# Expert stage: second layer two pairs behind the first, its result transposes beside the gather's

## The reference

```python
h = _layernorm(x) * (1.0 + sc2) + sh2
f = _moe_ffn(h, router_w, router_b, exp_w1, exp_w3, exp_w2, sh_w1, sh_w3, sh_w2)
x = _layernorm(DN_ALPHA * x + g2 * f, ln2_w, ln2_b)
```

## Time and profile before

| | |
|---|---|
| median of 3 runs | 2037.02 us (2030.13 to 2043.91) |
| profiled execution, first to last instruction | 2023.2 us |
| mean granted TensorE clock | 0.955 of full speed |
| TensorE busy | 1867.4 us, 92% of the span |
| VectorE, ScalarE, POOL busy | 980.9, 647.1, 331.0 us |
| first-layer matmuls (L3467), 1536 of them | 343.6 us |
| second-layer matmuls (L3451), 768 of them | 176.8 us |
| first matmul of the first pair, end of the last pair | 1381.4 us, 1980.6 us |

### The profile page before, as it was taken

The page is one execution under the profiler, slowest core; times in us unless marked ns, Lnnn a source line. Parts: engine busy times, 40 slices in busy tenths (PEclk is TensorE's granted clock), DMA queues, the critical chain, the costliest instruction groups (busy, mean ns, idle before and its releaser), DMA issues.

```text
span 2023.2 us, 33529 instructions
## 1 busy us (share of the span) xinstructions
PE 1867.4 (92%) x14234; PEld 1338.9 (66%) x14234; DVE 980.9 (48%) x1446; ACT 647.1 (32%) x1012; POOL 331.0 (16%) x316
## 2 busy tenths in 40 slices
PE   7989998999997999899999789979899999999991
PEld 6878998999997999765755679874333333333330
DVE  5745555465664677746545754663232222222116
ACT  5544334444454433420033532422111112111110
POOL 2100000000000100012200025402133233233323
PEclk9989999999998999999899789979999999999996
DMA  8534555544443877446497000076999999999885
GB/s 278 189 105 157 186 187 187 164 147 147 151 141 121 296 249 249 148 149 185 148 343 250 1 14 4 4 298 264 420 391 366 373 370 367 377 371 374 328 328 200
DMA packets 199700, 456.49 MB, mean 226 GB/s; under 512 B 33048, under 2 KB 154392, under 8 KB 170000
## 3 DMA queue, kind: packets, MB, share of 16 engines
q1 hardware_dynamic: 157104, 377.18, 51.8%
q0 software_dynamic: 35712, 57.73, 8.4%
q10 hardware_dynamic: 6752, 19.67, 2.7%
HBM read 549.91 MB, written 52.43 MB: 298 GB/s over the span
## 4 chain that ended last, share of the span: by engine, by line
PE 81%; DVE 8%; DMA 4%; issue 3%; ACT 3%; POOL 1%; SPq 0%; ACTq 0%; POOLq 0%; DVEq 0%
PE psum L349 32%; PE psum L3467 15%; PE psum L3451 7%; PE psum L1570 7%; PE psum L1577 2%; PE psum L3393 2%; DMA mem<-in_exp_w_dram 2%; PE psum L2607 2%; ACT w_hi L405 1%; PE psum L2591 1%; DVE w_lo L410 1%; DMA mem<-in_exp_w_dram,mem 1%; PE psum L3480 1%; PE psum L569 1%; PE psum L3150 1%
## 5 line engine op out<-in xcount | busy, mean ns | idle before, releaser
L410 DVE TENSOR_TENSOR w_lo<-mem,w_hi 128x2048 fp32r<-128x2048 f32 x122 | 280.2, 2299 | 228.0 <-ACT w_hi L405 225.4
L349 PE MATMUL psum<-x_hi,w_hi 128*128 128x256 f32 x1216 | 349.0, 287 | 4.3 <-DVE x_lo L556 4.3
L3467 PE MATMUL psum<-mem 128*64 128x512 f32 x1536 | 343.6, 600 | 6.1 <-DMA mem<-in_exp_w_dram 3.6
L349 PE MATMUL psum<-x_hi,w_lo 128*128 128x256 f32 x1216 | 343.9, 283 | 0.0
L349 PE MATMUL psum<-x_lo,w_hi 128*128 128x256 f32 x1216 | 342.9, 282 | 0.0
L405 ACT ACTIVATE w_hi<-mem 128x2048 fp32r<-128x2048 f32 x122 | 233.9, 1918 | 192.9 <-PE psum L349 189.8
L3467 PEld LDWEIGHTS psum<-mem 128*64 128x64 f32 x1536 | 106.8, 138 | 204.4 <-issue 195.0
L349 PEld LDWEIGHTS psum<-x_hi,w_hi 128*128 128x128 f32 x1216 | 233.2, 192 | 10.1 <-DVE w_lo L410 4.7
L349 PEld LDWEIGHTS psum<-x_lo,w_hi 128*128 128x128 f32 x1216 | 236.7, 195 | 0.6
L349 PEld LDWEIGHTS psum<-x_hi,w_lo 128*128 128x128 f32 x1216 | 235.7, 194 | 0.0
L3451 PE MATMUL psum<-mem 128*64 128x512 f32 x768 | 176.8, 602 | 4.2 <-issue 3.0
(11 more groups left out here) (512 smaller groups left out, 2848.9 us busy)
## 6 DMA issues: line engine op xcount, KB each, us to landing
mem<-in_exp_w_dram SPq DMA_DIRECT2D x192, 1024.0 KB
mem<-in_dil_w_qkv_dram SPq DMA_DIRECT2D x36, 1024.0 KB, 5.3
mem<-in_ada_w_dram POOLq DMA_DIRECT2D x48, 512.0 KB, 4.2
mem<-in_ffn_w_gate_dram SPq DMA_DIRECT2D x22, 1024.0 KB, 5.6
mem<-in_ffn_w_up_dram SPq DMA_DIRECT2D x22, 1024.0 KB, 5.6
mem<-in_ffn_w_down_dram SPq DMA_DIRECT2D x22, 1024.0 KB, 4.7
mem<-in_w_in_dram SPq DMA_DIRECT2D x13, 1024.0 KB, 5.5
mem<-in_na_w_qkv_dram SPq DMA_DIRECT2D x12, 1024.0 KB, 8.4
```

Source lines behind the costliest of these rows:

```text
L349: ins = pe.matmul(out, lhs[a], rhs[b], start=start and k == 0, stop=stop and k == 2, **kw)
L410: dve.tensor_tensor(w_lo[n % SLOTS][:, 0, :], ring[:, n % SLOTS, :], w_hi_f[n % HI][:, 0, :], ALU.subtract).then_inc(S("w_split"), 1)
L3467: ins = pe.matmul(psum[r, up, :].rearrange("p (a n) -> p a n", a=2), xg[:, b % 2, c, x * P + 64 * e:x * P + 64 * e + 64], w_up[s][e][:, :, ...
```

## The change

The second layer runs two pairs behind the first. In iteration k TensorE now runs the first layer of pair k, then at once the two result transposes of pair k-1 (`turned(k - 1)`), then the 8 gather transposes, then the second layer of pair k-2. `hid_T` gets a second buffer. VectorE copies the turned result of pair k-1 ahead of the product of pair k. All that belongs to the second layer moves along: SP issues, behind the first-layer loads of pair k, the second-layer loads of pair k-2 (it was k-1), POOL likewise for spare pairs, and `y_put` and `y_out` come an iteration or two later. The last two pairs are written out by hand.

```diff
-    hid_T = gain_b[:, 512:768].rearrange("p (c j) -> p c j", c=2)
+    hid_T = [gain_b[:, 512 + 256 * q:768 + 256 * q].rearrange("p (c j) -> p c j", c=2) for q in range(2)]
...
-        for k, (kind, n) in enumerate(PAIRS + [("end", 0)]):
+        for k, (kind, n) in enumerate(PAIRS + 2 * [("end", 0)]):
...
-            elif k >= 3 and PAIRS[k - 1][0] == "own":
-                sp.wait_ge(*at("mx_y", k - 2))
-                down_rows(k - 1, PAIRS[k - 1][1], range(2))
+            elif k >= 4 and PAIRS[k - 2][0] == "own":
+                sp.wait_ge(*at("mx_y", k - 3))
+                down_rows(k - 2, PAIRS[k - 2][1], range(2))
...
-            if k > 2 and PAIRS[k - 1][0] == "spare":
-                fetch_down(k - 1, PAIRS[k - 1][1])
+            if k > 3 and PAIRS[k - 2][0] == "spare":
+                fetch_down(k - 2, PAIRS[k - 2][1])
...
-            if k - 3 >= PLAIN:
-                y_put(pool, k - 3)
-        y_put(pool, len(PAIRS) - 3)
+            if k - 4 >= PLAIN:
+                y_put(pool, k - 4)
+        for k in range(len(PAIRS) - 4, len(PAIRS) - 2):
+            y_put(pool, k)
...
+        def turned(k):
+            pe.wait_ge(*at("mx_hid", k + 1))
+            after(pe, "hid_T", k)
+            if k == 0:
+                pe.wait_ge(*at("spare_rows", 3))
+            for f in range(2):
+                ins = pe.transpose(bank(1, P, f * P), hid_tok[:, f::2], ident)
+            ins.then_inc(S("hid_turned"), 1)
...
             ins.then_inc(S("mx_up"), 1)
+            if 0 < k < last:
+                turned(k - 1)
             if b + 1 < BATCHES:
                 for u in range(2):
                     gather_pe(pe, b + 1, 2 * x + u)
-            if k:
-                down(k - 1)
-            pe.wait_ge(*at("mx_hid", k + 1))
...
-            for f in range(2):
-                ins = pe.transpose(bank(1, P, f * P), hid_tok[:, f::2], ident)
-            ins.then_inc(S("hid_turned"), 1)
             if k == 0:
                 slot_toks_pe(pe, 2)
-        down(len(PAIRS) - 1)
+            if 2 <= k < last:
+                down(k - 2)
+            if k == last - 1:
+                turned(k)
+                down(k - 1)
+        down(last - 1)
+        turned(last)
+        down(last)
...
-            if k == 1:
+            if k == 3:
                 act.wait_ge(*at("y_filled", 16 * FILLS))
-            if 0 < k <= PLAIN:
-                y_out(act, k - 1)
+            if 3 <= k < 3 + PLAIN:
+                y_out(act, k - 3)
...
+        def hid_turned(k):
+            dve.wait_ge(*at("hid_turned", k + 1))
+            after(dve, "mx_y", k - 1)
+            dve.tensor_copy(hid_T[k % 2], bank(1, 256).rearrange("p (c j) -> p c j", c=2)).then_inc(S("hid_T"), 1)
+
         for k in range(len(PAIRS)):
             b, x = divmod(k, 2)
+            if 0 < k < last:
+                hid_turned(k - 1)
             dve.wait_ge(*at("mx_silu", k + 1))
             after(dve, "hid_turned", k)
             dve.tensor_tensor(hid_tok, sil, bank((0, 6)[k % 2], 256, 256), ALU.mult).then_inc(S("mx_hid"), 1)
-            if k:
+            if 2 <= k < last:
+                y_dve(dve, k - 2)
+            if k == last - 1:
+                hid_turned(k)
                 y_dve(dve, k - 1)
```

More of the change, by code:

```diff
@@ L3450, in down @@
                         r = slice(64 * e, 64 * e + 64)
-                        ins = pe.matmul(psum[r, 4 + h, :], hid_T[:, f, r], w_down[s][e][:, f, 512 * h:512 * h + 512],
+                        ins = pe.matmul(psum[r, 4 + h, :], hid_T[s][:, f, r], w_down[s][e][:, f, 512 * h:512 * h + 512],
                                         start=f == 0, stop=f == 1)
             ins.then_inc(S("mx_y"), 1)
+        def turned(k):
[6 more added lines that the diff above has]
+            ins.then_inc(S("hid_turned"), 1)
+        last = len(PAIRS) - 1
         for k in range(len(PAIRS)):
@@ L3473, in moe_pe @@
                     gather_pe(pe, b + 1, 2 * x + u)
-            if k:
-                down(k - 1)
-            pe.wait_ge(*at("mx_hid", k + 1))
-            if k == 0:
-                pe.wait_ge(*at("spare_rows", 3))
-            for f in range(2):
-                ins = pe.transpose(bank(1, P, f * P), hid_tok[:, f::2], ident)
-            ins.then_inc(S("hid_turned"), 1)
             if k == 0:
                 slot_toks_pe(pe, 2)
-        down(len(PAIRS) - 1)
+            if 2 <= k < last:
[6 more added lines that the diff above has]
+        down(last)
     def xg_act(act, b, u):
@@ L3548, in moe_dve @@
             dve.tensor_tensor(hid_tok, sil, bank((0, 6)[k % 2], 256, 256), ALU.mult).then_inc(S("mx_hid"), 1)
-            if k:
+            if 2 <= k < last:
+                y_dve(dve, k - 2)
+            if k == last - 1:
+                hid_turned(k)
                 y_dve(dve, k - 1)
-            dve.wait_ge(*at("hid_turned", k + 1))
-            after(dve, "mx_y", k)
-            dve.tensor_copy(hid_T, bank(1, 256).rearrange("p (c j) -> p c j", c=2)).then_inc(S("hid_T"), 1)
             if k == 0:
@@ L3564, in moe_dve @@
                 gate_dve(dve, k - 2)
-        y_dve(dve, len(PAIRS) - 1)
+        y_dve(dve, last - 1)
+        hid_turned(last)
+        y_dve(dve, last)
         for r in range(3):
```

## The result

The changed kernel takes 2040.7 us, the median of 20 runs, against 2030.8 us for the kernel before, also of 20. The ratio is 1.0054, with a 95% interval of 1.0036 to 1.0072: half a per cent slower, 11 us. (Three of the forty, at 2196 us and more, ran in a slow state and are left out of the ratio.) The forecast had the direction and the place, and three times the size: +34 us. (The three runs shown before the change had a median of 2037.0; with twenty it is 2030.8. A profiled execution of the changed kernel took 2040.27 us with a span of 2038.1, so what lies around the span is 2.2 us, not the 13.8 that I took over; the execution profiled before was a quick one: 2.2 us on its span of 2023.2 give 2025.4.)

The account below looks back on a forecast made before the run. TensorE's instructions were taken to bound the kernel, loads close behind. Load-loop and end terms of +25.0 us plus +9.4 for the clock gave +34 on the 2023.2 us span; with a 13.8 us offset, 2071 us, range 2038 to 2092.

Parts of the forecast that it names:

- The drains saved on TensorE: On TensorE between second and next first layer: 0.36 us saved on about 26 of 48 pairs, 9.4 us if TensorE stays the bound.
- The first rival: Turns of three pairs: ten loads land within 27.5 us, no wait appears, 9.4 us gained, 2028 us; chance 0.12.
- the second, the loop without the clock: Every third first layer: waits of 1.7 to 3.0 us, full clock, turns of 37.7 to 39.0 us, 2045 to 2062 us; chance 0.28.
- the signs that I named: Middle stretch: waits about 3 us every third pair, turns 38 to 41 us, TensorE share about 0.92, clock below 1.00.
- 30.4 + 1.4 us: Load loop of each turn: ten loads, 10.49 MB at 0.345 MB a us, 30.4 us, plus 1.4 for start and landing.
- My lower bound: Load loop of each turn: ten loads packed without a gap, with q0's small packets, take 29.2 us, a turn of 37.7.
- The upper bound of 41.5: Load loop of each turn: a 3.9 us tail at the end of the loads makes a turn 41.5 us.
- a small gain behind up(40): After pair 40's first layer, with fewer loads: TensorE saves 4 x 0.36 = 1.4 us.
- the clock at the 11 places: First layers after 3.0 us load waits: a clock halving costs 1.7 us, at half of 11 places, +9.4 us.
- gains nothing here: Second layer two pairs behind: its waits for results were already covered, TensorE idling 0.45 us in 365.66, so no gain.
- the loop from up(7) to up(40): First layers of pairs 7 to 40: 2.1 us lost up to pair 10, then ten turns losing 2.43 each, 24.3.

## Why the prediction was right or wrong

*Right: the place and the mechanism.* The drains saved on TensorE, the fixed times at a change between the two shapes of matmul (0.54 us a turn forecast, 0.52 measured, with the split between the pairs wrong) don't shorten the turn; d(k-2) ahead of u(k+1) makes every third first layer wait, and only those. Halving the load in front takes the waits away, a load more makes them longer, and the old distance removes them for the most part. The first rival (TensorE stays the bound, 2028 us) is out: it asked for ten loads in 27.5 us. Nearest came the second, the loop without the clock: full clock and waits at every third pair, but a turn of 37.04 us, below its 37.7 to 39.0. Of the signs that I named, the order on TensorE and the places of the waits came; turns of 38 to 41 us, a TensorE share of 0.92 (it is 0.97) and a clock below 1.00 did not.

*Wrong: the size of the loop.* The failed step is the term "30.4 + 1.4 us" for ten loads. Measured, a turn of 37.04 us less up's 7.1 leaves 29.9, not 31.8. In the turn shown above the first packet came 1.0 us behind up(13), and from there to the landing the queues did this:

```profile
GB/s 115 253 356 402 471 402 379 506 402 379 506 379 402 506 380 403 426 449 379 379 437 437 402 425 448 402 379 494 391 403 403 449 403 403 368 420 363 323 265 219
...
q1 hardware_dynamic: 1437, 10.46, 89.8%
```

These are 40 slices of 28.5 us: 10.46 MB, 0.367 MB a us, against the 0.345 of the earlier trace rows. The 0.345 was a mean over whole turns of the kernel before, and in them the queue has a weak spell: the row of slices in the earlier trace rows shows it, 265 to 346 GB/s around 1570 to 1576, where u(16) has only just been released (1571.17 in the earlier trace rows). The new order has d(13) in the queue at that moment, so inside the loop there is hardly such a spell; it has moved to where up(16) already runs:

```profile
GB/s 5 125 304 421 421 430 430 430 430 430 430 430 403 394 394 412 412 430 430 430 421 421 421 430 421 403 394 394 421 359 292 247 260 238 376 412 421 349 390 265
```

This is the window from 1567.4 to 1604.0, 0.91 us a slice; the spell (292, 247, 260, 238) begins at 1594.9, as u(16) finishes. My lower bound, 29.2 us packed and a turn of 37.7, was the nearer figure, and even it was a little high, for it put 1.4 us where 1.0 is seen, and 29.2 for loads that took 28.5 in this turn. (The upper bound of 41.5 sums to 41.4; nothing hangs on it.) The mean rate of the old order was the wrong row to price a stretch of the new one.

*Wrong by the same step: the clock.* The price was right (1.69 us, and on the loop). After waits of 2.7 to 4.1 us, in the kernel with one more load, eleven first layers of eleven ran partly at half clock; in the changed kernel, with waits of 1.0 us on the mean, 0 and 2 of 11 did, not 5 or 6. The Trainium skill ("TensorE: Matmul & The Clock Gate", section "HAM oscillation — how this bites in real kernels") has a wait ahead of each block put the array to half clock every time. The kernel with one more load agrees; the changed kernel's shorter waits are not that case.

*Missing: start and end.* I counted nothing ahead of up(10) ("the loads are the limit in both kernels") and a small gain behind up(40). The loads are the limit there, but a second layer two pairs behind releases its slots a pair later, the queues run dry twice, and two first layers that run partly at half clock (4.6 us) hold up the loads behind them; the start takes 5.1 us longer. I counted the clock at the 11 places only. The second layer that no longer fits into the start's waits is paid at the end, 3.2 us net of the saved drains. All five profiles at a distance of two have 90.0 to 92.2 us and 102.8 to 105.1 us in these stretches, all five at a distance of one 85.9 to 87.3 and 98.2 to 99.6. My sentence that the greater distance "gains nothing here" should have been followed by what it costs: one pair more in the pipe.

By terms: the loop from up(7) to up(40) +4.5 where 26.4 was forecast, the clock at the 11 places 0 to 3.4 where 9.4, start +5.1 where 0, end +3.2 where -1.4. The direction came out of one term that was more than five times too large and two that I had not counted. So it is in part luck: the turns alone cost 4.5 us, 0.2%.

## What to carry to other kernels

When a consumer is moved back by a stage, write out the order in which the loads leave the queue and find the closed loop: what release starts a burst, which loads stand in it, and which work at its end frees the next. Price that burst with the rate of a stretch in which the queue is never empty, not with a mean over turns that holds the old order's dry spells. A deeper pipe also has to be filled and emptied: here 8.3 of the 12.8 us lie in the start and the end, where the forecast had counted no loss. And the edit's useful half needed no greater distance at all.

## What the runs showed of the hardware

A run of ten transposes between two blocks of 64-column matmuls takes 1.34 us if the two from on-chip results come first and 1.45 if they come last (0.35 + 0.99 against 1.01 + 0.44, start to start), with the same instructions. And from up(10) to up(40) waits of 1.94, 1.99 and 2.03 us were each followed by a first layer partly at half clock (8.78 us for 7.09), while 1.88 and less were not; near the start a wait of 2.59 us was, while 2.15, 2.33 and 2.65 us ahead of first layers were not. What tells these apart was not tried.
